# Gate and up projections of four feed-forward layers by one level of Strassen's scheme, seven block products in place of eight

## What is computed

```python
x = x + 0.5 * swiglu(rms_norm(x), w_gate, w_up, w_down)   # D_MODEL 1024, D_FF 2816
x = x + mixer(rms_norm(x))       # layer 0: gMLP spatial gating; layer 1: latent attention with a paged cache
x = x + 0.5 * swiglu(rms_norm(x), w_gate, w_up, w_down)

def swiglu(h, w_gate, w_up, w_down):
    return (silu(h @ w_gate) * (h @ w_up)) @ w_down
```

## Time and profile before

| | |
|---|---|
| median of 3 runs | 2261.16 us (2260.68 to 2262.51) |
| the profiled execution | 2261.99 us; span of its trace 2260.3 us |
| PE busy | 2229.8 us, 99% (18020 matmuls) |
| DVE busy | 913.3 us, 40% |
| ACT busy | 712.3 us, 32% |
| POOL busy | 433.1 us, 19% |
| chain that ended last | PE 95%, DVE 2%, POOL 1%, ACT 1% |
| granted TensorE clock | 0.996 of full speed |
| traffic with memory | 198.73 MB, mean 88 GB/s |

### The profile page before, as it was taken

The page is one execution under the profiler, slowest core; times in us unless marked ns, Lnnn a source line. Parts: engine busy times, 40 slices in busy tenths (PEclk is TensorE's granted clock), DMA queues, the critical chain, the costliest instruction groups (busy, mean ns, idle before and its releaser), DMA issues.

```text
span 2260.3 us, 42702 instructions
## 1 busy us (share of the span) xinstructions
PE 2229.8 (99%) x18020; PEld 2155.1 (95%) x18020; DVE 913.3 (40%) x1112; ACT 712.3 (32%) x893; POOL 433.1 (19%) x371
## 2 busy tenths in 40 slices
PE   9999999999999999999999999999999999999999
PEld 8999999999999999999999999987668789999999
DVE  5333334335354333333433333477655543323333
ACT  5212223433233212223321222444553433212122
POOL 1202112213132202112220201223121122102020
PEclk9999999999999999999999999999999999999999
DMA  5222222332222222222222222331222112222222
GB/s 176 93 93 93 93 89 79 94 93 69 83 76 94 93 93 93 93 92 76 94 93 93 93 93 89 109 101 40 74 89 71 38 57 93 94 93 93 93 84 66
DMA packets 203622, 198.73 MB, mean 88 GB/s; under 512 B 12071, under 2 KB 200788, under 8 KB 203252
## 3 DMA queue, kind: packets, MB, share of 16 engines
q1 hardware_dynamic: 202938, 196.67, 27.3%
q10 hardware_dynamic: 314, 0.37, 0.1%
q0 software_dynamic: 256, 0.07, 0.0%
HBM read 194.42 MB, written 2.66 MB: 87 GB/s over the span
## 4 chain that ended last, share of the span: by engine, by line
PE 95%; DVE 2%; POOL 1%; ACT 1%; issue 1%; DMA 0%; SPq 0%; POOLq 0%; DVEq 0%; ACTq 0%
PE main L622 81%; PE side L1134 2%; PE main L906 1%; PE side L622 1%; PE side L1101 1%; PE side L937 1%; PE main L1064 1%; PE side L990 1%; PE main L969 1%; PE side L825 1%; PE main L716 1%; PE main L1051 1%; POOL h_lo L2022 0%; PE main L1052 0%; PE main L1053 0%
## 5 line engine op out<-in xcount | busy, mean ns | idle before, releaser
L622 PE MATMUL main<-xg_hi,w_hi 128*128 128x260 f32 x3296 | 666.1, 283 | 0.8 <-DVE x L1544 0.8
L622 PE MATMUL main<-xg_hi,w_lo 128*128 128x260 f32 x3296 | 664.9, 283 | 0.0
L622 PE MATMUL main<-xg_lo,w_hi 128*128 128x260 f32 x3296 | 663.5, 283 | 0.0
L1520 DVE TENSOR_TENSOR w_lo<-raw,w_hi 128x2048 fp32r<-128x2048 f32 x166 | 380.6, 2293 | 363.1 <-ACT w_hi L1164 359.6
L622 PEld LDWEIGHTS main<-xg_hi,w_hi 128*128 128x128 f32 x3296 | 508.9, 189 | 1.6 <-DVE x L1544 1.0
L622 PEld LDWEIGHTS main<-xg_hi,w_lo 128*128 128x128 f32 x3296 | 508.8, 189 | 0.0
L622 PEld LDWEIGHTS main<-xg_lo,w_hi 128*128 128x128 f32 x3296 | 507.2, 188 | 0.0
L1164 ACT ACTIVATE w_hi<-raw 128x2048 fp32r<-128x2048 f32 x162 | 308.6, 1905 | 345.2 <-PE main L622 345.2
L622 PE MATMUL main<-h_hi,w_hi 128*128 128x260 f32 x1920 | 387.3, 283 | 2.9 <-POOL h_lo L2022 2.9
L622 PE MATMUL main<-h_hi,w_lo 128*128 128x260 f32 x1920 | 386.9, 283 | 0.0
L622 PE MATMUL main<-h_lo,w_hi 128*128 128x260 f32 x1920 | 385.8, 282 | 0.0
(11 more groups left out here) (304 smaller groups left out, 1583.8 us busy)
## 6 DMA issues: line engine op xcount, KB each, us to landing
raw<-in_ffn_w_up SPq DMA_DIRECT2D x44, 1024.0 KB, 5.2
raw<-in_ffn_w_gate SPq DMA_DIRECT2D x43, 1024.0 KB, 5.2
raw<-in_ffn_w_down SPq DMA_DIRECT2D x32, 1024.0 KB, 4.9
raw<-in_gmlp_w_in SPq DMA_DIRECT2D x16, 1024.0 KB, 5.5
raw<-in_ffn_w_down SPq DMA_DIRECT2D x16, 768.0 KB, 4.2
raw<-in_gmlp_w_out SPq DMA_DIRECT2D x8, 1024.0 KB, 5.0
raw<-in_mla_w_o SPq DMA_DIRECT2D x8, 1024.0 KB, 5.0
over<-in_cache_mla SPq DMA_DIRECT2D x64, 104.0 KB, 2.0
```

What stands on the lines that cost most here:

```text
L622: mm = nc.tensor.matmul(into[:, half, 0:HALF], w[:, k, m * P:(m + 1) * P], moving[:, k, half * HALF:(half + 1) * HALF], start=(k == 0 and ...
L1520: nc.vector.tensor_tensor(w_lo[:, 1 - s, :], raw[:, 1 - s, :], w_hi[:, 1 - s, :].bitcast(F32), ALU.subtract).then_inc(lo_done, 1)
```

## The change

In each gate or up chunk the product (256 columns) x (1024 contraction) x (520 tokens) is seen as 2x2 blocks times 2x2 blocks: the output's two 128-column tiles, the even and the odd contraction tiles, the two token halves. Eight block products (4 contraction tiles each, 12 matmuls of 260 columns with the three operand combinations) become seven, in the form with few additions: four weight sums `sums_w` per chunk, made by DVE (`sums_outer`, `sums_second`, `sums_last`); sums of activation blocks (`blocks`), made once per FFN for each pair of x tiles by ACT and DVE (`fast_norm`, in place of `norm_tile` where an FFN follows), split into `xw_hi`/`xw_lo` (7 blocks x 4 x 260 columns). ACT's part of it: from a tile's high half x gain to `xw_hi` (260 words, then 260 more when DVE has the difference), for the second tile a scaled copy of 260 and one of 520 words, and at the end one of 780. The results are combined through PSUM: a block named `summed` (a bank of `side`, alternating by chunk) takes products j = 0, 2, 4 and 6 (of 0 to 6) on top of one another, and ACT copies its state after 0 and after 2, and the bank of product 1, to `snap`; DVE adds or subtracts. So a chunk has 84 matmuls.

- PE: `fast_chunk` with waits per product. The weight split comes in pieces of 512 or 1024 words a partition: five ACT copies and five DVE subtractions per chunk.
- The first two pairs of FFN 0 stay as they were, 84 of 88 gate and up chunks are changed. FFN 0 also makes the `xw` blocks of its own third pair on (`norm_pair`).
- POOL's tmp_mul = tmp_act x rstd is gone. h is kept without the factor, and the down tiles get it instead: `scaled_to_x` is two DVE instructions, where `add_to_x` was one. (The down tiles of the mixers keep `add_to_x`.)
- `FF_GROUPS = (3, 4, 4)`. Some semaphores are merged. The loads' waits are counted anew (`free`), and the trig and page table loads at FFN 2's end also wait for its last addition to x.
- The gMLP, the attention, and the matmuls of `down` are the same.

The core of the diff (the bookkeeping of counts is left out):

```diff
-FF_GROUPS = (4, 4, 3)
+FF_GROUPS = (3, 4, 4)
...
+            def fast_chunk(s, e, l, sn, x_waits=None, between=None):
+                summed, other, alone = side[:, s, 0:HALF], main[:, 0, 0, 0:HALF], main[:, 0, 1, 0:HALF]
+                into = (summed, other, summed, alone, summed, other, summed)
+                ready = (l + 1, l + 2, None, l + 3, l + 4, None, l + 5)
+                for j in range(7):
+                    if ready[j] is not None:
+                        pe.wait_ge(lo_done, ready[j])
+                    if j == 0:
+                        pe.wait_ge(evac_done, e - 4)
+                    elif j == 1:
+                        pe.wait_ge(evac_done, e - 1)
+                    elif j == 2:
+                        pe.wait_ge(snapped, sn + 1)
+                    elif j == 4:
+                        pe.wait_ge(snapped, sn + 3)
+                    elif j == 6:
+                        pe.wait_ge(evac_done, e + 2)
+                    if between and j in between:
+                        between[j]()
+                    for k in range(4):
+                        if x_waits and (j, k) in x_waits:
+                            pe.wait_ge(xg_lo_done, x_waits[j, k])
+                        for i, (w, moving) in enumerate(((w_hi, xw_hi), (w_hi, xw_lo), (w_lo, xw_hi))):
+                            mm = nc.tensor.matmul(into[j], w_tiles(w, j)[:, k, :], moving[:, k, j, :],
+                                                  start=(j in (0, 1, 3) and k == 0 and i == 0), stop=(k == 3 and i == 2),
+                                                  skip_group_check=True)
+                    mm.then_inc(tile_done, 1)
...
+            def fast_chunk(s, raw_ready, t, e, w, after, middle=None):
+                act.wait_ge(tile_done, t + 1)
+                act.wait_ge(evac_done, e - 3)
+                nc.scalar.activation(snap[:, 0, :], side[:, s, 0:HALF], ACT.Copy).then_inc(snapped, 1)
+                nc.scalar.activation(w_tiles(w_hi, 6), raw_parts(s)[:, 3], ACT.Copy).then_inc(hi_done, 1)
+                act.wait_ge(tile_done, t + 2)
+                act.wait_ge(evac_done, e - 2)
+                nc.scalar.activation(snap[:, 1, :], main[:, 0, 0, 0:HALF], ACT.Copy, scale=-1.0).then_inc(snapped, 1)
+                act.wait_ge(raw_in[1 - s], raw_ready)
+                if after == "fast":
+                    nc.scalar.activation(w_tiles(w_hi, 0), raw_parts(1 - s)[:, 0], ACT.Copy).then_inc(hi_done, 1)
...
+                act.wait_ge(tile_done, t + 3)
+                act.wait_ge(evac_done, e - 1)
+                nc.scalar.activation(snap[:, 2, :], side[:, s, 0:HALF], ACT.Copy).then_inc(snapped, 1)
+                if after == "fast":
+                    act.wait_ge(weights_summed, w + 5)
+                    nc.scalar.activation(w_block(w_hi, 1, 2), sums_w[:, 2:4, :].rearrange("p a c -> p (a c)"),
+                                         ACT.Copy).then_inc(hi_done, 1)
+                act.wait_ge(tile_done, t + 4)
+                if after == "fast":
+                    nc.scalar.activation(w_tiles(w_hi, 3), raw_parts(1 - s)[:, 2], ACT.Copy).then_inc(hi_done, 1)
+                    if middle:
+                        middle()
+                    fast_third(t + 6, w + 3)
...
+            def sums_outer(s, raw_ready, rested=None):
+                dve.wait_ge(raw_in[s], raw_ready)
+                if rested is not None:
+                    dve.wait_ge(lo_done, rested)
+                parts = raw_parts(s)
+                nc.vector.tensor_tensor(sums_w[:, 0:4:2, :].rearrange("p a (i c) -> p a i c", c=P), parts[:, 0:4:3],
+                                        parts[:, 1:2].to_broadcast([P, 2, 4, P]), ALU.add).then_inc(weights_summed, 1)
...
+            def rest_raw(s, j, r, l):
+                dve.wait_ge(hi_done, l)
+                take_rest(w_tiles(w_lo, j), raw_parts(s)[:, r], w_tiles(w_hi, j), lo_done)
+            def rest_sums(j, at, l):
+                dve.wait_ge(hi_done, l)
+                take_rest(w_block(w_lo, j, 2), sums_w[:, at:at + 2, :].rearrange("p a c -> p (a c)"), w_block(w_hi, j, 2), lo_done)
...
+            def fast_chunk(s, raw_ready, t, e, l, w, sn, ro, into, by, after, before_rows=None):
+                if after == "fast":
+                    sums_outer(1 - s, raw_ready, l + 4)
+                rest_raw(s, 6, 3, l + 5)
+                if after == "fast":
+                    sums_second(1 - s, w + 3)
+                    rest_raw(1 - s, 0, 0, l + 6)
+                    sums_last(1 - s, w + 3)
...
+                summed, other, alone = side[:, s, 0:HALF], main[:, 0, 0, 0:HALF], main[:, 0, 1, 0:HALF]
+                low, high = slice(0, HALF), slice(HALF, TOK)
+                dve.wait_ge(tile_done, t + 4)
+                dve.wait_ge(snapped, sn + 1)
+                nc.vector.tensor_tensor(into[:, 0, low], alone, snap[:, 0, :], ALU.add).then_inc(evac_done, 1)
+                if after == "fast":
+                    rest_sums(1, 2, l + 7)
+                dve.wait_ge(tile_done, t + 5)
+                dve.wait_ge(snapped, sn + 2)
+                nc.vector.tensor_tensor(into[:, 1, high], snap[:, 1, :], summed, ALU.subtract).then_inc(evac_done, 1)
+                if after == "fast":
+                    rest_raw(1 - s, 3, 2, l + 8)
...
+                dve.wait_ge(tile_done, t + 6)
+                dve.wait_ge(snapped, sn + 3)
+                nc.vector.tensor_tensor(into[:, 0, high], other, snap[:, 2, :], ALU.add).then_inc(evac_done, 1)
+                if before_rows:
+                    before_rows()
+                dve.wait_ge(evac_done, e + 3)
+                nc.vector.tensor_tensor(into[:, 0, :], into[:, 0, :], by[0], ALU.mult).then_inc(row_set, 1)
+                dve.wait_ge(tile_done, t + 7)
+                nc.vector.scalar_tensor_tensor(into[:, 1, low], summed, -1.0, by[1][:, low], ALU.mult,
+                                               ALU.mult).then_inc(evac_done, 1)
+                nc.vector.tensor_tensor(into[:, 1, high], into[:, 1, high], by[1][:, high], ALU.mult).then_inc(row_set, 1)
+                if after == "fast":
+                    rest_sums(4, 0, l + 9)
...
+                else:
+                    dve.wait_ge(xg_hi_done, hi + 1)
+                    nc.vector.scalar_tensor_tensor(blocks[:, 3, :], x[:, 2 * i + 1, hi_half], gains[1], blocks[:, 0, :],
+                                                   ALU.mult, ALU.subtract).then_inc(block_set, 1)
+                    dve.wait_ge(block_set, b + 1)
+                    nc.vector.scalar_tensor_tensor(blocks[:, 2, :], x[:, 2 * i, lo_half], minus[0], blocks[:, 3, :],
...
+                    dve.wait_ge(block_set, b + 3)
+                    dve.wait_ge(xg_hi_done, hi + 2)
+                    take_rest(xw_lo[:, i, 2:7:2, :], blocks[:, 2:5, :], xw_hi[:, i, 2:7:2, :], xg_lo_done)
+            def scaled_to_x(k, m, t, ro):
+                dve.wait_ge(tile_done, t)
+                nc.vector.tensor_tensor(halves(tmp_mul[:, m, :]), main[:, m, :, 0:HALF], halves(rstd_all[:, :]),
+                                        ALU.mult).then_inc(row_set, 1)
+                dve.wait_ge(row_set, ro)
+                nc.vector.scalar_tensor_tensor(x[:, k, :], tmp_mul[:, m, :], 0.5, x[:, k, :], ALU.mult, ALU.add).then_inc(evac_done, 1)
...
                         for m in range(2):
-                            pool.wait_ge(act_done, a + 2 * i + m + 1)
-                            nc.gpsimd.tensor_tensor(tmp_mul[:, m, :], tmp_act[:, m, :], rstd_all[:],
-                                                    ALU.mult).then_inc(mul_done, 1)
...
```

More of the change, by code:

```diff
@@ L416, in program @@
         at_wo = at_uq.past(chunk=4, tile=24, evac=24)
-        at_ffn[3] = at_wo.past(chunk=8, tile=16, evac=16, h=H, norm=1, sums=KD)
+        at_ffn[3] = at_wo.past(chunk=8, tile=16, evac=16, h=H, norm=1, sums=KD, xg=KD)
         P_AT = [0, 1, 3, 6]
@@ new lines, in ffn @@
+                    rest = pairs
+                    if g == 0 and at.chunk == 0:
+                        first_pair()
+                        spread_first()
+                        for m in range(2):
+                            before = {}
+                            if m == 0:
+                                before = {0: lambda: pe.wait_ge(piece_lo, KD), 2: lambda: pe.wait_ge(piece_lo, KD + 1),
+                                          4: lambda: pe.wait_ge(piece_lo, KD + 2), 6: lambda: pe.wait_ge(lo_done, 2)}
+                            out_tile(m, 1, KD, start_hi, start_lo, before=before,
+                                     **(dict(into=side[:, 0:2, :]) if m == 0 else dict(free=e + 2)))
+                        for s in range(2):
+                            pe.wait_ge(lo_done, l + 3 + s)
+                            for m in range(2):
+                                out_tile(m, s, KD, start_hi, start_lo, free=e + ((2, 4), (5, 6))[s][m])
+                        e, l, rest = e + 8, l + 4, pairs - 2
+                        gate_up(0, True, e, l)
```

(8 more changed lines are left out.)

579 lines of the change are left out of this document (385 added, 194 removed).

## The result

| | before | after |
|---|---|---|
| median | 2260.92 us (2258.45 to 2262.51, 4 runs) | 2220.89 us (2218.38 to 2221.83, 4 runs) |
| span of the profiled execution | 2260.3 us | 2218.3 us |
| granted TensorE clock, mean | 0.996 | 0.991 |
| PE's matmuls | 18020 | 17012 |

The ratio is 0.9822, 95% interval [0.9805, 0.9839]: 40 us or 1.8% faster, where 68 us were forecast. The time lies inside the range of 2158 to 2238 us, but above the 2171 to 2211 of the forecast's own case. 28 us of the gain are missing.

The account below looks back on a forecast made before the run. PE's matmul count was taken as the bound; 2262.0 - 121.1 + 24 + 17 + 8 + 2 + 2.2 = 2194.1 us, with the median 0.8 lower: 2193 us, 3.0% faster. The 8-in-10 range was 2158 to 2238 us.

Parts of the forecast that it names:

- PE, -121.1: Gate and up chunks: 84 matmuls at an unchanged pace save 1.442 us a chunk, 84 times, -121.1 us.
- Rival D: Saving not had: seven products into one bank run slower than 120 ns each, or loads come late; 2315 us; chance 0.02.
- A steady chunk: DVE's queue in a steady changed chunk takes 8.8 us and fits into PE's 10.1 us.
- Rival B: Steady chunks: DVE is partly the bound, a chunk lasts 10.2 to 10.4 us; about 2215 to 2245 us; chance 0.18.
- The port, +24: Pairs: POOL's h_lo delays DVE through the shared port, PE stands 0.8 us, 30 times; +24 us (9 to 36).
- Entries, +17: Entries of FFN 1, 2, 3: PE waits for DVE's x blocks and POOL's square sums delay them; +17 us (10 to 23).
- the clock has nothing to give: Whole kernel: granted clock over 0.9 in all forty slices, so no term for the clock was in the sum.
- Reciprocal, +8: First chunk of FFN 1, 2, 3: the 3.40 us reciprocal on DVE makes PE stand 0.7 then 2.0 us; +8 for three.
- FFN 0, +2: FFN 0: DVE finishes the first pair's blocks and chunk 2's rest at 42.1, PE finishes chunk 1 at 40.2; +2 us.
- Small ends, +2.2: `scaled_to_x`'s extra 0.7 us instruction shows behind the last tile before gMLP, before attention and at the end; +2.2 us.
- rival A: PE never waits for the new work: locks at 0, half the entries, one reciprocal; 2156 us; chance 0.12.
- C: Slower: DVE limits steady chunks and POOL's two instructions cost their full 2.6 us in each pair; 2278 us; chance 0.07.

Follow-up runs that it names:

- experiment 3: Changed kernel with h_lo of the gate and up pairs made by DVE at the pair's end instead of by POOL; 2185.99 us, ratio 0.9676.
- Experiment 2: Changed kernel with a second POOL subtraction of 512 words into a spare buffer ahead of each h_lo of FFN 1, 2 and 3; 2369.65 us, ratio 1.047.
- experiments 1: Changed kernel with POOL's h_lo subtraction cut to 8 of 520 columns and down products taking h_hi for h_lo; 2180.38 us, ratio 0.9641.
- experiment 7: Changed kernel with POOL's additions of squares cut to 8 of 520 columns; 2207.16 us, ratio 0.9761.
- experiment 5: Changed kernel with ACT taking the first snap and last two weight blocks before copying the last x blocks, at entries of FFN 1, 2, 3; 2223.14 us.
- Experiment 9: Changed kernel with 36 and 44 extra PE matmuls into an unused bank before the snap wait at the entries of FFN 1 and 2; 2216.61 us.
- experiment 11: Changed kernel with pair h_lo on DVE, product 4's bank read before the 1024-word remainder, and extra PE matmuls in entry waits of FFN 1, 2, 3; 2181.67 us.
- Experiment 8: Changed kernel with the reciprocal of the token scales on 8 of 520 columns in every stage that has one; 2213.80 us, ratio 0.9795.

## Why the prediction came out as it did

**PE, -121.1: right.** 84 matmuls a chunk at 0.120 us, twelve in a row into one bank in 1.44 us. The row with two matmuls into one bank had pointed the right way. Rival D is out.

**A steady chunk: right.** A 1024-word subtraction holds DVE for 1.14 us (854.57 to 855.71 in experiment 3), 512-word ones begin 0.60 apart (839.79, 840.39 and 841.00 in the changed kernel), the queue of 8.8 us fits into 10.1, and the pair without POOL is 20.20 us, PE's own time. Rival B, in which DVE is the bound, is refuted by experiment 3: DVE took on 1.2 us of new work a pair and the kernel became faster. The measured time lies among B's numbers (2215 to 2245) all the same, which says nothing for its cause. What was wrong here is the figure for DVE's busy time, 1450 against 1564: 63 us of the difference are the stretched instructions (252 x (819 - 683) + 84 x (1568 - 1225) ns).

**The port, +24: right mechanism and place, too small.** The 30 pauses are 1.1 us each, 33 us. I had 1.2 as the bound "if POOL gets in at once both times", and took 0.8, by the row of the attention stage in which a single instruction met it. The bound was what happened: POOL does get in both times. Experiment 2 shows why: when both engines have a queue of such work they take turns, one instruction each, and every POOL instruction of 1.31 us costs DVE 1.0 to 1.1. The nearest row had only one of each and could not show that. The Trainium skill's rule (SBUF — State Buffer, Who interferes with whom) is borne out by experiments 1, 2, 3 and 7; that it spoke against the change was right. The lock was worth 33 us in the pairs and some 9 in the entries.

**Entries, +17: 21 us of pauses, and a slower pace that the sum had at nothing.** The chain of DVE was sized well: 14.0 us for the last chunk of FFN 2 plus the port, measured 15.5 with it and 13.9 without (experiment 7); both square sums hit it and not one. Two steps failed. First, "PE can do two products and three quarters of the third": PE did two, since the third adds to the bank whose snap ACT takes only behind the copy of the last blocks. I had followed the operands and not the accumulator. By experiment 5 it is worth 1.5 us in FFN 1 and nothing in sum elsewhere. Second, "the clock has nothing to give" was read from a kernel whose PE hardly stands in the FFNs; the change makes it stand, and then the clock has something to take. The matmuls at 1.2 GHz cost 2.4, 3.4 and 4.1 us in FFN 1, 2 and 3, the places behind the other pauses of their first chunks included, 10 us in all. With the first intervals behind the pauses, 4.4 us, that makes 14, the largest missing term. Experiment 9 shows the cause for the clock's part in FFN 1 and for part of it in FFN 2; FFN 3 is argued by likeness, since experiment 11's matmuls came too late there. The prediction had called itself wrong if entries cost over 10 us each: pauses and clock before the reciprocal together are 8.7, 14.0 and 6.6 us.

The Trainium skill has this case too (TensorE: Matmul & The Clock Gate, HAM oscillation — how this bites in real kernels): a wait of some length puts PE back to the low clock and each such wait pays again. In experiment 2 22 of 24 waits paid. I had not weighed it, though the trace of before has a small case, at the start of the gMLP, which the forty slices average away. PE waits 0.7 us for POOL's sum of squares and does twelve matmuls of 1 to 8 columns, and 1.4 us after it is back at L622 14 matmuls of that line begin 0.217 us apart (columns as in rows 3):

```profile
499.20:502.30 3.10, 3.10 (x16) 3.10 (x16) 0.76 (x3) 0.75 (x1) 0.00 (x0) 0.50 0.33 58
```

**Reciprocal, +8: 6.** Experiment 8. **FFN 0, +2: 4.6 and an extra lock.** 1.2 us is the pause foreseen, behind the rest of the first chunks; 2.5 and 0.9 us, ahead of the first changed chunk's products (DVE's reading of the last plain tile and the snap), were not in the list. The extra lock is a pause of 1.7 us for DVE's second reading at 78 us. **Small ends, +2.2**: the waits ahead of `rms` at the gMLP's and the attention's entry are 1.5 us where they were 0.8, as said; the third doesn't show (from the last down matmul to the end 7.5 us, before 7.4).

**The sum.** 33 for 24, 21 for 17, 14 for 0, 6 for 8, 4.6 for 2, 1.4 for 2.2: 26.8 us more than forecast, where 28 are missing. That it closes so well is partly luck: the extra lock of 1.7 us isn't in it, and the 21 us hold 1.0 that the kernel before paid at FFN 3's entry too. The profiled execution is 2220.5; rival A had 2156, C 2278. C's condition, more than 3.0 us in a pair, is met in experiment 2 (4.8 us a pair over 20.2), and that kernel is slower than before.

## What to carry to other kernels

When work is moved to VectorE, look at what GpSimd does at that moment, not how busy either is: two queues of SBUF-to-SBUF work side by side take turns, one instruction each, and it may pay to give GpSimd's small work to VectorE as well. Ask of a late reading whether the engine is short of time or only does something else first; a swap of two instructions gave half of what GpSimd's part cost back. And when a change makes TensorE stand for several microseconds where it never stood, price the slow matmuls behind the pause too.
